# Handing over from the opening to the gather stream seven half turns earlier

## The chip, the cores and the metric

One core of a Trainium2 chip. The metric is the device time of one execution, in microseconds.

## The reference

One layer over 1024 prompt tokens and 64 sample tokens, float32, width 1024. Both kinds of token go through the mixer, then through the expert channel.

```python
xn = rmsnorm(x)                         # mixer
z = xn @ w_in                           # u (512), conv in (1024), gates (2048)
a = glu(gelu(s5(u)));  b = conv_module(z_conv) @ w_conv_out
x = x + (sigmoid(g_a) * a + sigmoid(g_b) * b) @ w_out
q = rmsnorm(x) @ w_q                    # 8 heads x 2 halves of 128
s1, s2 = q1 @ keys1.T, q2 @ keys2.T     # 128 scores each
v1, i1 = top_k(s1, 16);  v2, i2 = top_k(s2, 16)
sc, pos = top_k(v1[:, None] + v2[None, :], 16)    # 16 experts of 16384
coef = softmax(sc) * gelu(u_tab[e] @ xn)          # dot with the expert's u row
x = x + sum_k coef[k] * v_tab[e[k]];  y = rmsnorm(x)
```

So every token and head needs 16 expert rows of 8 KB (u and v side by side), gathered by index.

## The kernel before

**Two streams of work.** The mixer works on four groups of 272 tokens (256 of the prompt, 16 of the sample), channel-major. The expert channel works on nine tiles of 128 rows: tiles 0 to 7 are the prompt, two to a group, and tile 8 holds the sample tokens twice, half of the heads each. While the experts of group g are gathered, the mixer of group g+1 runs beside them.

**Turns.** A *slot* is one gathered block of 128 rows x 8 KB (1 MB), one expert per token of the tile. A *pair* is two heads, so 32 slots. A *turn* is 4 slots; 8 turns a pair (`PTURNS`), 32 turns a prompt tile, 64 turns a group, 272 turns in all (1088 slots). Each turn has two *half turns*, and the pieces of the mixer are dealt out to half turns by a table written by hand: `OPENING` for group 0, `STEADY` for groups 1 to 3. `mix_half` maps the running half-turn number to (h, group): the first `2 * SKEW` numbers go to the rest of the opening, h = OPEN, OPEN+1 and so on, and the next is h = 0 of group 1.

**The opening.** Half turns h = 0 to OPEN-1 of group 0 run with no slots beside them. All five engines walk the same list, each in its own program order, with semaphores between them. Late in it come: h 42 to 49, the eight `out` slabs (x + m @ w_out on TensorE, copied out by ScalarE with two instructions, L905 and L906); `rows`, the transposes of the result back to token rows (`token_rows`, TensorE L769, copied by `keep_rows`, VectorE L1317); `q`, sixteen query slabs, h 50 to 65 (16 matmul records of 272 columns, L591, copied by ScalarE into `qT`, L919); `score`, three key products (L708) which read that copy, one per query slab, copied out by `keep_scores` (L853, L854). ScalarE also does `sq` (sums of squares, L910, L911) and `rs` (L914, L916, after a root on GpSimd, L1608), which give `rst`, the row scale of the softmax and of `xn`.

**Choosing.** `made_top` (unit = 4 * head + 2 * half + tile) takes the top 16 of 128 scores with seven VectorE instructions; `tops` holds its half turns. `pair_top` takes the top 16 of 256 sums, `experts_of` turns positions into indices `idx` (L1439). `choose(n, r)` does both for the two heads of pair n in turns r = 2, 3, 6, 7 of the pair before. For pair 0 they are done in the opening, at h = CHOICE, both heads in a row. `exps` (ScalarE, Exp) and `weights` (VectorE) make the softmax weights `soft` of a pair.

**A slot's way.** GpSimd issues the gather (L1642) into one of 8 buffers (`RING`), two turns ahead, when TensorE has freed the buffer. VectorE does `dot` with `xn` (L1463), ScalarE `batch` for two slots (Gelu, coefficient, diagonal matrix: L945, L948, L952), TensorE `slots` multiplies the diagonal by the v half and accumulates (L779, four records a slot).

**Order inside a turn.** TensorE: mixer half turn, 2 slots, mixer half turn, 2 slots. VectorE the same, with dots, then `choose`. ScalarE: batch, half turn, batch, half turn. In turn 0 (and every 32nd) it differs: TensorE does both half turns before its four slots; VectorE does the half turn, `xn`, `weights`, four dots, and then the second half turn; and ScalarE does:

```python
if turn % 32 == 0:
    beside(2 * turn)
    pair_start(n, r)
    batch(n, TB * r)
...
batch(n, TB * r + 1)
...
beside(2 * turn + 1)
```

**PSUM.** The tiles of `q`, `score` and `out` share two banks in turn (`a_tile` waits until the tile before the last was copied out); `rows` uses three others (`v_tile`). SyncE loads each weight slab (512 KB) four ahead, when TensorE has finished with the buffer.

Of the kernel before, what the change touches and what calls it, by code (L numbers as in the profile page):

```python
# [90 lines left out]
class Plan:  # L91
# [20 lines left out]
    def due(self, step, h):  # L112
# [9 lines left out]
     "rows": [51, 52], "rest": [], "q": [50 + m for m in range(2 * HEADS)],  # L122
     "score": [51 + m for m in range(2 * HEADS)]},
# [4 lines left out]
     "cout": [38, 39, 40, 41], "rows": [52, 53], "sq": [53], "ms2": [54], "rs": [55],  # L128
     "tops": [52 + u // 2 for u in range(2 * HEADS)] + [64 + u for u in range(2 * HEADS)],
# [25 lines left out]
SKEW = 3  # L155
LAGS_AT = 12
CHOICE = 55
CHOSEN = 59
OPEN = 61
# [32 lines left out]
def program(nc, x_prompt, x_sample, kept, first, slabs, experts, g_ffn, g_final, x2_d, rs_d, score_d, made_d,  # L192
# [5 lines left out]
    with ExitStack() as ctx:  # L198
# [359 lines left out]
        def _(pe):  # L558
# [153 lines left out]
            def mix(h, g):  # L712
# [39 lines left out]
                for j in at("rows", h):  # L752
                    if j == 0:
                        a_emptied(a_at(g, "out", DT - 1))
                    token_rows(v_at(g, "rows", j), SPANS[2 * j])
# [7 lines left out]
            def token_rows(v, span):  # L763

                n, width = span
                for c in range(2):
                    out = v_tile(v + c)
                    for m in range(4):
                        last = pe.transpose(out[0:width, m * P:(m + 1) * P], outT[:, 4 * c + m, n:n + width], eye)  # L769
                    last.then_inc(v_ready, 1)  # L770
# [12 lines left out]
            def beside(number):  # L783

                if mix_half(number):
                    mix(*mix_half(number))
                g = rest_of("make", number)
                if g is not None:
                    token_rows(rest_v(g), SPANS[1])
# [22 lines left out]
        def _(act):  # L812
# [112 lines left out]

            def exps(n):

                act.wait_ge(best_done, 2 * n + 2)
                t = n // TPAIRS
                if t < TILES:  # L930
                    act.wait_ge(rst_ready, t + 1)
                else:
                    act.wait_ge(rs_in, 32)
                act.activation(neg_top[:, :], best[:, :, 0], ACT.Copy, scale=rst[:, t % 2, 1:2]).then_inc(neg_done, 1)
                act.wait_ge(neg_done, n + 1)
                for a in range(2):
                    act.activation(ex[:, a, :], best[:, a, :], ACT.Exp, bias=neg_top[:, a:a + 1],
                                   scale=rst[:, t % 2, 0:1],
                                   accum_out=den[:, a:a + 1]).then_inc(exp_done, 1)
# [14 lines left out]
            def pair_start(n, r):  # L954
                if r == 0:
                    act.wait_ge(soft_done, n + 1)
                if r == PTURNS - 1 and n < LAST_PAIR:
                    exps(n + 1)
# [41 lines left out]
            for h in range(OPEN):  # L1000
# [13 lines left out]
                if h == CHOSEN:  # L1014
                    exps(0)
                mix(h, 0)
            for turn in range(ALL_TURNS):
# [16 lines left out]
        def _(dve):  # L1034
# [423 lines left out]

            def dot(n, s0, s1):
# [63 lines left out]
            for h in range(OPEN):  # L1523
                if h == LAGS_AT:
                    setup_lags()
                mix(h, 0)
                for unit, g in tops_of(h - OPEN):
                    made_top(unit, g)
                if h == CHOICE:
                    for r in range(PTURNS):  # L1530
                        choose(0, r)
            dve.wait_ge(norms_in, 16)
            for turn in range(ALL_TURNS):
# [6 lines left out]
                if r == 0:  # L1540
                    weights(n)
                if turn % 32 == 0:
                    dot(n, STEPS * r, STEPS * (r + 1))
                    if ended_at(turn) is not None:
                        end(ended_at(turn))
                    if n < LAST_PAIR:
                        choose(n + 1, r)
                    beside(2 * turn + 1)
                else:
                    dot(n, STEPS * r, STEPS * r + BATCH)  # L1550
                    beside(2 * turn + 1)
                    dot(n, STEPS * r + BATCH, STEPS * (r + 1))
                    if n < LAST_PAIR:
# [204 lines left out]
```

## Time and profile before

| | |
|---|---|
| median of 3 runs | 3399.02 us (3393.8 to 3400.26) |
| profiled execution, first to last instruction | 3400.9 us (the page has no other time of it) |
| TensorE busy | 92% |
| VectorE / ScalarE / GpSimd busy | 71% / 36% / 42% |
| DMA | 1311.20 MB, mean 386 GB/s; 1140.92 MB of it in the gathers' queue |
| granted TensorE clock, mean | 0.985 |
| first gather issued | 289.22 us |
| first slot's matmuls | 315.71 us |
| half turn 0 of group 1 begins on TensorE | 352.60 us |

Instruction times in the timeline are starts from the beginning of the span. Consecutive instructions of a kind are merged; "x16" counts records. A float32 matmul leaves two records, so a query slab has 16 (eight products). "idle before <- X" is the time that the engine waited and what released it. The 4 us windows give the granted clock of just that stretch.

### The profile page before, as it was taken

What the parts mean: (1) busy time and instruction counts of PE and PEld (TensorE: products, weight loads), DVE (VectorE), ACT (ScalarE), POOL (GpSimd) and SP (SyncE); (2) the same over time, 40 slices, a digit from 0 to 9 for tenths busy, and PEclk for the clock granted to TensorE, in tenths of its full rate; (3) what the DMA queues carried; (4) which work ended last, traced back from release to release, by engine and by line L of the source; (5) the groups of instructions that cost most, each with busy time, mean ns of one, the idle gap of its engine ahead of it and who ended that gap; (6) DMA issues with size and microseconds to landing.
All of it is one profiled execution on the core that took longest, in us unless ns stands there. A gap on an engine that the chain in (4) does not pass through costs nothing.

```text
span 3400.9 us, 33356 instructions
## 1 busy us (share of the span) xinstructions
PE 3120.6 (92%) x10016; PEld 1785.7 (53%) x10016; DVE 2420.6 (71%) x5476; ACT 1218.7 (36%) x4064; POOL 1417.0 (42%) x1244
## 2 busy tenths in 40 slices
PE   8999999999999999999999999999998777777776
PEld 6877566555555565655554665655554223222232
DVE  8826998766578798665678798665688666666664
ACT  4323443343333443343334443333333333233332
POOL 1201355443344355343434454343434554454443
PEclk9999999999999999999999999999999999999999
DMA  4357999999999999999999999999999999999998
GB/s 133 103 181 284 369 403 418 419 411 419 417 402 416 405 415 417 418 412 418 412 415 413 396 418 413 394 419 419 412 410 384 420 420 420 394 420 420 419 403 341
DMA packets 209604, 1311.20 MB, mean 386 GB/s; under 512 B 23632, under 2 KB 28880, under 8 KB 70160
## 3 DMA queue, kind: packets, MB, share of 16 engines
q0 software_dynamic: 156672, 1140.92, 81.9%
q1 hardware_dynamic: 51472, 167.36, 13.0%
q8 instruction: 80, 1.31, 0.2%
q10 hardware_dynamic: 1280, 0.79, 0.1%
q14 instruction: 100, 0.82, 0.1%
HBM read 1298.34 MB, written 10.64 MB: 385 GB/s over the span
## 4 chain that ended last, share of the span: by engine, by line
PE 60%; DMA 21%; DVE 10%; issue 4%; ACT 3%; POOL 2%; POOLq 0%; DVEq 0%; SPq 0%; ACTq 0%
PE ps_acc L779 34%; DMA rows<-in_experts,idx 21%; PE ps_a L591 15%; DVE rows L1463 4%; PE ps_a L681 4%; PE ps_v L591 4%; POOL rows L1642 2%; PE ps_a L708 1%; PE ps_y L648 1%; ACT coef L948 1%; PE ps_a L685 1%; ACT diag L952 1%; PE ps_v L630 1%; DVE va L1297 1%; PE ps_v L692 0%
## 5 line engine op out<-in xcount | busy, mean ns | idle before, releaser
L779 PE MATMUL ps_acc<-rows,diag 128*128 128x512 f32 x4352 | 1998.5, 608 | 244.2 <-ACT diag L952 242.0
L1642 POOL DMA_INDIRECT rows<-in_experts,idx x1088 | 1290.5, 1186 | 1714.5 <-PE ps_acc L779 1377.6
L1463 DVE CUSTOM_DVE_ANT_0 rows<-rows,xn 128x1024 f32<-128x1024 f32 x1088 | 1324.9, 1230 | 776.3 <-DMA rows<-in_experts,idx 766.5
L779 PEld LDWEIGHTS ps_acc<-rows,diag 128*128 128x128 f32 x4352 | 818.2, 193 | 1275.6 <-issue 861.3
L945 ACT ACTIVATE act_v<-dots 128x2 f32<-128x2 f32 x544 | 110.6, 203 | 1789.6 <-DVE dots L1463 1787.7
L952 ACT ACTIVATE diag<-pk,coef 128x128 f32<-128x128 f32 x1088 | 377.2, 394 | 17.7
L591 PE MATMUL ps_a<-xnT,ring 128*128 128x272 f32 x1536 | 374.1, 399 | 0.9 <-issue 0.8
L591 PEld LDWEIGHTS ps_a<-xnT,ring 128*128 128x128 f32 x1536 | 295.9, 193 | 92.6 <-issue 33.9
L948 ACT ACTIVATE coef<-act_v,soft 128x1 f32<-128x1 f32 x1088 | 261.4, 287 | 17.8
L1297 DVE SCALAR_TENSOR_TENSOR va<-va,pk 128x302 f32<-128x302 f32 x480 | 258.8, 601 | 0.5
L591 PE MATMUL ps_a<-gates,ring 128*128 128x272 f32 x1024 | 246.3, 394 | 0.9 <-ACT gates L906 0.9
L591 PEld LDWEIGHTS ps_a<-gates,ring 128*128 128x128 f32 x1024 | 193.5, 190 | 63.0 <-issue 24.4
L681 PE MATMUL ps_a<-xnT,ring 128*128 128x272 f32 x512 | 130.3, 399 | 2.4 <-DVE xnT L1374 1.2
L591 PE MATMUL ps_v<-uy,ring 128*128 128x272 f32 x512 | 124.7, 392 | 0.0
L681 PEld LDWEIGHTS ps_a<-xnT,ring 128*128 128x128 f32 x512 | 94.5, 190 | 31.0 <-issue 11.5
L591 PEld LDWEIGHTS ps_v<-uy,ring 128*128 128x128 f32 x512 | 97.3, 190 | 24.9 <-issue 5.7
L1463 DVE DVE_READ_ACCUMULATOR2_ANT dots<- 128x1 f32 x1088 | 88.7, 82 | 0.0
L1608 POOL TENSOR_TENSOR rs<-rs,half 128x3 f32<-128x3 f32 x4 | 3.7, 931 | 153.9 <-DVE rs L1244 153.8
L591 PE MATMUL ps_a<-uy,ring 128*128 128x272 f32 x256 | 64.0, 393 | 0.5 <-ACT uy L839 0.5
L839 ACT ACTIVATE uy<-ps_a 32x68 f32<-32x68 f32 x256 | 56.0, 219 | 22.9 <-PE ps_a L591 19.9
L591 PE MATMUL ps_v<-xnT,ring 128*128 128x272 f32 x256 | 61.4, 393 | 0.0
L708 PE MATMUL ps_a<-pk,sig 128*128 128x128 f32 (+1 forms) x384 | 59.5, 276 | 0.0
(268 smaller groups left out, 2003.1 us busy)
## 6 DMA issues: line engine op xcount, KB each, us to landing
ring<-in_slabs SPq DMA_DIRECT2D x256, 512.0 KB
rows<-in_experts,idx POOLq DMA_INDIRECT x1088
ring<-made_slabs SPq DMA_DIRECT2D x24, 512.0 KB
xt<-in_x_prompt SPq DMA_DIRECT2D x4, 1024.0 KB, 13.2
out_y_prompt<-yt SPq DMA_DIRECT2D x8, 512.0 KB, 8.6
ring<-made_slabs SPq DMA_DIRECT2D x12, 256.0 KB
made_slabs<-rows SPq DMA_DIRECT2D x1, 2048.0 KB, 9.6
made_slabs<-rows SPq DMA_DIRECT2D x4, 512.0 KB, 9.3
```

Of the source, the lines that this page charges most:

```text
L591: last = pe.matmul(out[:, 0:N], w, rhs[:, k, :], start=(k == 0), stop=(k == kt - 1))
L630: last = pe.matmul(out[:, i * NK:(i + 1) * NK], w, uS[:, t, i * NK:(i + 1) * NK], start=True, stop=True)
L681: last = pe.matmul(out[:, 0:N], ring[:, slot, k * P:(k + 1) * P], merged[:, k, :], start=(k == 0), stop=(k == DT - 1))
L708: last = pe.matmul(out[0:width, t * KEYS:(t + 1) * KEYS], qT[:, m % 2, n:n + width], keys, start=True, stop=True)
L779: ins = pe.matmul(ps_acc[:, h, :], diag[:, slot, :], rows[:, slot, D + h * 512:D + (h + 1) * 512], start=first, stop=False, skip_group_che ...
L839: last = act.activation(o, x, func)
L945: act.activation(act_v[:, cols], dots[:, cols], ACT.Gelu).then_inc(gelu_done, 1)
L948: act.activation(coef[:, s:s + 1], act_v[:, s:s + 1], ACT.Copy, scale=soft[:, n % 2, s:s + 1]).then_inc(coef_done, 1)
L952: act.activation(diag[:, s % RING, :], shape, ACT.Copy, scale=coef[:, s:s + 1]).then_inc(diag_done, 1)
L1297: last = dve.scalar_tensor_tensor(acc[:, c, :], src, wk, acc[:, c, :], ALU.mult, ALU.add)
L1463: ins = dve.tensor_tensor_reduce(rows[:, slot, 0:D], rows[:, slot, 0:D], xn[:, :], 1.0, 0.0, ALU.mult, ALU.add, dots[:, s:s + 1])
L1642: pool.indirect_dma_start(out=rows[:, slot, :], out_offset=None, in_=experts, in_offset=bass.IndirectOffsetOnAxis(ap=idx[:, a, k:k + 1], a ...
```

## The change

Seven things move. The turns with slots begin at half turn 54, not 61, and `SKEW` goes from 3 to 6, so 12 half turns of the opening (54 to 65) lie beside slots instead of 6 (61 to 66), and group 1 begins at turn 6 instead of turn 3. `rows` moves from 51, 52 to 49, 50, ahead of the first query, and each half of it now waits only for the `out` slabs that it reads; `sq`, `ms2` and `rs` follow to 50 and 51. The scores of a head, both halves, are now made in one half turn, right behind the second query. The units of head 0 and 1 for tile 0 go first in `tops`. Head 0 of pair 0 is chosen at h = 51 and weighted by itself (`first_exps`, `first_weights`); head 1 is chosen in turns 0 and 1 and weighted in turn 3.

```diff
--- before.py
+++ after.py
@@ -119,14 +119,14 @@
      "s": [10, 12, 14, 16], "y": [15, 18, 21, 24],
      "gate": [13 + m for m in range(14)] + [35, 36], "glu": [27 + j for j in range(DT)],
      "mean": [29], "var": [31], "cout": [37, 38, 39, 40], "out": [42 + j for j in range(DT)],
-     "rows": [51, 52], "rest": [], "q": [50 + m for m in range(2 * HEADS)],
-     "score": [51 + m for m in range(2 * HEADS)]},
+     "rows": [49, 50], "rest": [], "q": [50 + m for m in range(2 * HEADS)],
+     "score": [51 + m - m % 2 for m in range(2 * HEADS)]},
     {"cp": [7, 9, 11, 13], "turn_in": [11, 13, 15, 17], "scan": [11, 13, 15, 17], "turn_back": [11, 13, 15, 17],
      "gelu": [16, 19, 22, 25], "tap": [10, 10, 12, 12, 14, 14, 16, 16] + [18 + u // 2 for u in range(24)],
      "glu": [28 + j for j in range(DT)],
      "centre": [30], "square": [30], "eps": [32], "root": [32], "scale": [33], "swish": [34],
-     "cout": [38, 39, 40, 41], "rows": [52, 53], "sq": [53], "ms2": [54], "rs": [55],
-     "tops": [52 + u // 2 for u in range(2 * HEADS)] + [64 + u for u in range(2 * HEADS)],
+     "cout": [38, 39, 40, 41], "rows": [49, 50], "sq": [50], "ms2": [51], "rs": [51],
+     "tops": [51, 54, 51, 55, 53, 57, 53, 58, 56, 60, 56, 61, 58, 62, 59, 63] + [64 + u for u in range(2 * HEADS)],
      "load_x": [59], "sq_next": [63], "ms_next": [64], "norm_next": [65]}, False, 0)
 STEADY = Plan(
     {"xn": [0, 1, 2, 3], "u": [9, 11, 21, 23], "cq": [5, 7, 13, 17], "cp": [6, 8, 15, 19],
@@ -152,11 +152,11 @@
 SLABS_0, SLABS_G = len(OPENING.slabs), len(STEADY.slabs)
 SLABS = SLABS_0 + (GROUPS - 1) * SLABS_G
 
-SKEW = 3
+SKEW = 6
 LAGS_AT = 12
-CHOICE = 55
-CHOSEN = 59
-OPEN = 61
+CHOICE = 51
+FIRST_EXPS = 3
+OPEN = 54
 ALL_TURNS = TILES * TPAIRS * PTURNS + SPAIRS * PTURNS
 LAST_PAIR = TILES * TPAIRS + SPAIRS - 1
 
@@ -750,9 +750,7 @@
                         pe.wait_ge(merged_done, DT * (g + 1))
                     out_slab(j, g)
                 for j in at("rows", h):
-                    if j == 0:
-                        a_emptied(a_at(g, "out", DT - 1))
-                    token_rows(v_at(g, "rows", j), SPANS[2 * j])
+                    token_rows(v_at(g, "rows", j), SPANS[2 * j], g)
                 for m in at("q", h):
                     if m == 0:
                         a_emptied(a_at(g, "out", DT - 1))
@@ -760,11 +758,12 @@
                 for m in at("score", h):
                     scores(m, g)
 
-            def token_rows(v, span):
+            def token_rows(v, span, g):
 
                 n, width = span
                 for c in range(2):
                     out = v_tile(v + c)
+                    a_emptied(a_at(g, "out", 4 * c + 3))
                     for m in range(4):
                         last = pe.transpose(out[0:width, m * P:(m + 1) * P], outT[:, 4 * c + m, n:n + width], eye)
                     last.then_inc(v_ready, 1)
@@ -786,7 +785,7 @@
                     mix(*mix_half(number))
                 g = rest_of("make", number)
                 if g is not None:
-                    token_rows(rest_v(g), SPANS[1])
+                    token_rows(rest_v(g), SPANS[1], g)
 
             pe.wait_ge(kept_in, 16)
             pe.sem_inc(slot_free, RING)
@@ -923,6 +922,15 @@
                     act.wait_ge(x_in, 32 * (g + 2))
                     squares()
 
+            def first_exps(a):
+
+                act.wait_ge(best_done, a + 1)
+                act.wait_ge(rst_ready, 1)
+                act.activation(neg_top[:, a:a + 1], best[:, a, 0:1], ACT.Copy, scale=rst[:, 0, 1:2]).then_inc(neg_done, 1)
+                act.wait_ge(neg_done, a + 1)
+                act.activation(ex[:, a, :], best[:, a, :], ACT.Exp, bias=neg_top[:, a:a + 1], scale=rst[:, 0, 0:1],
+                               accum_out=den[:, a:a + 1]).then_inc(exp_done, 1)
+
             def exps(n):
 
                 act.wait_ge(best_done, 2 * n + 2)
@@ -932,7 +940,7 @@
                 else:
                     act.wait_ge(rs_in, 32)
                 act.activation(neg_top[:, :], best[:, :, 0], ACT.Copy, scale=rst[:, t % 2, 1:2]).then_inc(neg_done, 1)
-                act.wait_ge(neg_done, n + 1)
+                act.wait_ge(neg_done, n + 2)
                 for a in range(2):
                     act.activation(ex[:, a, :], best[:, a, :], ACT.Exp, bias=neg_top[:, a:a + 1],
                                    scale=rst[:, t % 2, 0:1],
@@ -952,8 +960,12 @@
                     act.activation(diag[:, s % RING, :], shape, ACT.Copy, scale=coef[:, s:s + 1]).then_inc(diag_done, 1)
 
             def pair_start(n, r):
+                if n == 0 and r == FIRST_EXPS:
+                    first_exps(1)
+                if n == 0 and r == PTURNS // 2:
+                    act.wait_ge(soft_done, 2)
                 if r == 0:
-                    act.wait_ge(soft_done, n + 1)
+                    act.wait_ge(soft_done, n + 2 if n else 1)
                 if r == PTURNS - 1 and n < LAST_PAIR:
                     exps(n + 1)
 
@@ -1011,9 +1023,8 @@
                             last = act.activation(wt[W32 * k:W32 * (k + 1), i:PAIRS:CT, W32 * s:P],
                                                   lag[W32 * i:W32 * (i + 1), :, 0:width], ACT.Copy)
                     last.then_inc(wt_done, 1)
-                if h == CHOSEN:
-                    exps(0)
                 mix(h, 0)
+            first_exps(0)
             for turn in range(ALL_TURNS):
                 (n, r), t = divmod(turn, PTURNS), ended_at(turn)
                 if turn % 32 == 0:
@@ -1456,6 +1467,13 @@
                 dve.tensor_tensor(soft[:, n % 2, :].rearrange("p (a k) -> p a k", a=2), ex[:, :, :],
                                   inv[:, :].unsqueeze(2).to_broadcast([P, 2, TOPK]), ALU.mult).then_inc(soft_done, 1)
 
+            def first_weights(a):
+
+                dve.wait_ge(exp_done, a + 1)
+                step(dve.reciprocal(inv[:, a:a + 1], den[:, a:a + 1]))
+                dve.tensor_scalar(soft[:, 0, a * TOPK:(a + 1) * TOPK], ex[:, a, :], inv[:, a:a + 1], None,
+                                  ALU.mult).then_inc(soft_done, 1)
+
             def dot(n, s0, s1):
                 for s in range(s0, s1):
                     slot = s % RING
@@ -1527,8 +1545,8 @@
                 for unit, g in tops_of(h - OPEN):
                     made_top(unit, g)
                 if h == CHOICE:
-                    for r in range(PTURNS):
-                        choose(0, r)
+                    pair_top(0, 0)
+                    experts_of(0, 0)
             dve.wait_ge(norms_in, 16)
             for turn in range(ALL_TURNS):
                 n, r = divmod(turn, PTURNS)
@@ -1537,12 +1555,16 @@
                 beside(2 * turn)
                 if turn % 32 == 0:
                     start(turn // 32)
-                if r == 0:
+                if n == 0 and r in (0, FIRST_EXPS):
+                    first_weights(r // FIRST_EXPS)
+                if r == 0 and n:
                     weights(n)
                 if turn % 32 == 0:
                     dot(n, STEPS * r, STEPS * (r + 1))
                     if ended_at(turn) is not None:
                         end(ended_at(turn))
+                    if n == 0:
+                        pair_top(0, 1)
                     if n < LAST_PAIR:
                         choose(n + 1, r)
                     beside(2 * turn + 1)
@@ -1550,6 +1572,8 @@
                     dot(n, STEPS * r, STEPS * r + BATCH)
                     beside(2 * turn + 1)
                     dot(n, STEPS * r + BATCH, STEPS * (r + 1))
+                    if (n, r) == (0, 1):
+                        experts_of(0, 1)
                     if n < LAST_PAIR:
                         choose(n + 1, r)
                 if turn > 32 and turn % 32 == 1:
```

## Rows read from the trace of the kernel before

**Rows 1.** The page: transfers in 40 slices, and the chain that ended last.

```profile
DMA  4357999999999999999999999999999999999998
...
PE 60%; DMA 21%; DVE 10%; issue 4%; ACT 3%; POOL 2%; POOLq 0%; DVEq 0%; SPq 0%; ACTq 0%
```

**Rows 2.** Stretches of 100 us: busy times, granted clock, DMA share, GB/s.

```profile
core 0: us, PE busy (x) PEld busy (x) DVE busy (x) ACT busy (x) POOL busy (x), PEclk, DMA share, GB/s
300.00:400.00 100.00, 94.38 (x338) 57.06 (x337) 78.75 (x241) 41.39 (x134) 31.07 (x28) 1.00 0.98 386
...
2800.00:2900.00 100.00, 76.78 (x160) 30.05 (x160) 63.96 (x127) 34.50 (x112) 47.41 (x41) 0.97 1.01 420
```

**Rows 3.** Stretches of 4 us in the first turns, same columns.

```profile
292.00:296.00 4.00, 4.00 (x19) 3.37 (x20) 3.73 (x13) 0.66 (x3) 3.08 (x4) 1.00 0.98 400
...
340.00:344.00 4.00, 4.00 (x19) 3.23 (x18) 3.83 (x13) 1.38 (x5) 2.15 (x2) 1.00 0.66 212
```

**Rows 4.** Line 1491, at the start of turns 224 and 256: durations, then first and last start.

```profile
L1491 DVE SCALAR_TENSOR_TENSOR xn<-x2t,rst,gf x1: 1277/1277/1277, 2897.7 to 2897.7; 128x1024 f32<-128x1024 f32 x1
...
L1491 DVE SCALAR_TENSOR_TENSOR xn<-x2t,rst,gf x1: 1284/1284/1284, 3226.8 to 3226.8; 128x1024 f32<-128x1024 f32 x1
```

**Rows 5.** VectorE in order of time: start, duration, line, idle before.

```profile
264.01 0.29 DVE L1391 MAX8 topv<-gp 128x8 f32<-128x128 f32 x1 [4.15 <-ACT gp L854]
...
265.85 0.29 DVE L1391 MAX8 topv<-gp 128x8 f32<-128x128 f32 x1
...
282.54 0.43 DVE L1417 TENSOR_TENSOR hot<-topv 128x256 f32<-128x256 f32 x1
...
288.08 0.18 DVE L1439 SCALAR_TENSOR_TENSOR idx<-part 128x16 uint32<-128x16 f32 x1
...
331.07 0.17 DVE L1244 TENSOR_SCALAR rstd<-ssq 128x3 f32<-128x3 f32 x1 [13.36 <-ACT hst L821]
```

**Rows 6.** TensorE in order of time, half turns 50 to 66 of the opening.

```profile
254.17 3.93 PE L591 MATMUL ps_a<-gates,ring 128*128 128x272 f32 x16 [0.87 <-ACT gates L906]
...
257.94 1.04 PE L769 MATMUL ps_v<-pk,gates 128*128 128x128 f32 x8
...
273.38 3.93 PE L591 MATMUL ps_a<-gates,ring 128*128 128x272 f32 x16
...
278.01 3.93 PE L591 MATMUL ps_a<-gates,ring 128*128 128x272 f32 x16
...
315.71 7.13 PE L779 MATMUL ps_acc<-rows,diag 128*128 128x512 f32 x16 [0.53 <-ACT diag L952]
...
322.68 3.83 PE L591 MATMUL ps_a<-gates,ring 128*128 128x272 f32 x16
...
336.60 3.70 PE L779 MATMUL ps_acc<-rows,diag 128*128 128x512 f32 x8 [1.26 <-ACT diag L952]
...
352.60 0.38 PE L600 MATMUL ps_a<-pk,va 128*128 128x128 f32 x2
```

**Rows 7.** GpSimd in order of time: the first gather.

```profile
289.22 1.19 POOL L1642 DMA_INDIRECT rows<-in_experts,idx  x1 [14.88 <-DVE idx L1439]
```

**Rows 8.** Line 455, the load of x: issue to landing, four transfers.

```profile
DMA to landing us min/median/max: 5.4/13.2/14.8
```

**Rows 9.** ScalarE in order of time.

```profile
270.28 1.06 ACT L910 ACTIVATE va<-x2t 128x1024 f32<-128x1024 f32 x1 [0.90 <-ACT gp L854]
...
313.21 1.28 ACT L945 ACT_TABLE_LOAD   x1 [2.01 <-DVE dots L1463]
...
317.19 0.38 ACT L919 ACTIVATE sig<-ps_a 128x272 f32<-128x272 f32 x1
```

**Rows 10.** Stretches of 4 us around a stop of TensorE at 110 us.

```profile
108.00:112.00 4.00, 2.10 (x14) 1.56 (x12) 3.83 (x10) 3.45 (x15) 0.21 (x1) 1.00 0.44 145
112.00:116.00 4.00, 4.00 (x22) 3.77 (x22) 4.00 (x7) 0.00 (x0) 2.70 (x3) 0.63 0.06 23
116.00:120.00 4.00, 4.00 (x10) 2.95 (x10) 4.00 (x7) 0.00 (x0) 3.40 (x5) 0.52 0.00 0
```

## Prediction

> **What bounds the kernel now.** I read four views in this order: the page, stretches of 100 us and 4 us, the timeline of each engine between 250 and 355 us, and single lines where a turn begins.
>
> The page shows two resources near their limit at once. The transfers fill nearly every slice from 300 us on, yet the chain that ended last lies 60% on TensorE and only 21% on transfers [rows 1]. The stretches part the two. At the end, with no mixer beside the slots, TensorE is busy 77% and the transfers run at 420 GB/s: there the gathers bound. In the first turns TensorE is busy 94% and the transfers reach 386 GB/s [rows 2]. In 4 us stretches: 400 GB/s when eight gathers have just been issued, but 212 GB/s at 340 us, where TensorE works all the time, the eight buffers are full, and no new gather can be issued until it frees one [rows 3]. So where query slabs run beside slots, TensorE bounds.
>
> Hence two prices. A turn without mixer costs (3226.8 - 2897.7) / 32 = 10.28 us [rows 4]. The same four slots cost TensorE 322.68 - 315.71 = 6.97 us [rows 6]; a query slab with its score costs it 278.01 - 273.38 = 4.63 us [rows 6].
>
> **The change, part by part.**
>
> *Where it acts.* From half turn 0 of group 1 on, table, costs and order are the same in both kernels, and only eight buffers carry anything over. So I take that stretch as equally long, and need two numbers: when TensorE reaches that half turn (352.60 us now [rows 6]), and what is left behind it. Left are three turns fewer, and they go missing at the end, where the mixer is over: 3 x 10.28 = 30.8 us. The change wins if TensorE gets there less than 30.8 us later.
>
> *`rows` ahead of the query.* The two transposes cost 1.04 us each [rows 6] and are only moved. The last `out` is done at about 253.3 us, since query 0 now waits 0.87 us to 254.17 [rows 6] for its copy. New: first half of the transposes inside that wait, the second behind it, then the sample rows, query 0 at 255.5, and by query 4 TensorE stands at 273.7 against 273.38 now: +0.3 us. ScalarE's `sq` now stands in front of the copy of query 0 (2.2 us from 270.28 [rows 9]), with the store of the sample rows ahead of it: it starts at about 257.2 and ends at 259.4, when query 0 has just ended. GpSimd's root and `rs` end at 261.4, before query 1 ends at 262.9. Covered; with slower row copies the scores would slip by as much.
>
> *The first gather.* Scores 0 and 1 come out of TensorE at 263.8 and 264.6, ScalarE has copied them at 264.5 and 265.4. Two units of `made_top` at 265.85 - 264.01 = 1.84 us each [rows 5] end at 268.3; `pair_top` with `experts_of` took 288.26 - 282.54 = 5.7 us [rows 5]: index at 274.0. Plus 0.96 us as now (288.26 to 289.22 [rows 5, 7]): gather at 275.0, 14.2 us earlier.
>
> *Turn 0, the new wait.* TensorE does half turns 54 and 55 and then the slots. In 55 lie query 5, score 4 and score 5, and score 5 needs ScalarE's copy of query 5. ScalarE makes that copy in its second half turn, behind both batches, and the second batch needs dots 2 and 3, so gathers 2 and 3. Now it is already so late (copy of query 12 at 317.19, after the batches [rows 9]), but there the half turn's score belongs to the query before and nobody waits. Query 5 ends at 281.1, score 4 at 281.9. Gather 0 lands no sooner than 275.0 + 5.4 = 280.4, the shortest time to landing of a load of that size [rows 8]. Gather 3 is three times 1.05 MB later, 2.5 us each at 420 GB/s [rows 2], and two slabs share the engines, 1.25 us each: 290.4. Dot, batch and copy: 1.15 + 1.4 + 0.5, so score 5 starts at about 293.4: TensorE stands 11.5 us. Bounds: 8 us if no slab shares (and dot 3 waits for nothing else), 15 us if the landing is as slow as the median 13.2 us of that load [rows 8], which was under full traffic. I take 11.5, since the engines are nearly empty at 275 us. Behind the copy on ScalarE wait the copies of scores 4 and 5, and behind these VectorE's units 8 and 10 in turn 1; they end at 299.3, before TensorE needs dots 4 and 5. The Gelu table load of 1.28 us [rows 9] is under the wait for gather 1.
>
> *Second head in turns 0, 1 and 3.* VectorE's work is the same plus two small instructions; it has room (12 of the 16 us of a turn). But ScalarE's `first_exps` in turn 3 loads the Exp table and then Gelu again, 1.28 us each, and comes only after the copy of score 9: I get dots 12 and 13 at 335.5, their diagonal at 338.3, TensorE free at 336.4: 1.9 us, 0 to 4.
>
> *Squares of the next x.* ScalarE does these 3.3 us at h = 63, behind scores 12 and 13, and VectorE waits for them before any dot (13.36 us now, which leads to a TensorE wait of 1.26 us [rows 5, 6]). After: VectorE waits until 367.3 in turn 5, dots 20 and 21 at 371.8, diagonal at 373.4, TensorE free at 370.4: 3.0 us, 1 to 5.
>
> *TensorE's ledger, query 4 to group 1.* Before: 12 queries with scores 55.6, one more score 0.9, three turns of slots 20.9, waits 0.53 + 1.26 = 1.8: 79.2, as the trace has it (352.60 - 273.38 [rows 6]). After: 55.6, six turns of slots 41.8, waits 11.5 + 1.9 + 3.0 = 16.4: 113.8, from 273.7: 387.5 us, so 34.9 us later than before.
>
> *The clock.* A stop as long is not cheap afterwards. At 110 us TensorE stood some 2 us and then ran 8 us at a granted 0.63 and 0.52, half of the time and more at 1.2 GHz [rows 10]; that lost 4 x (0.37 + 0.48) = 3.4 us. The waits of 0.5 to 1.3 us in the first turns cost nothing (clock 1.00 [rows 2]). I add 3.4 us for turn 0 and nothing for turns 3 and 5; bounds 0 and 7.
> The Trainium skill, TensorE: Matmul & The Clock Gate, section Why this matters for your kernels, says that an idle gap between bursts of matmuls brings the array back to half clock; by this rule the wait of turn 5 would fall under it too, and the sum would be some 3 us higher. The trace agrees for the 2 us stop at 110 us.
>
> *Credit.* In the first half turns of group 1 VectorE bounds (two units and four dots a turn), and it now enters them with nothing in hand, since its 13.36 us wait came 21.5 us before. After, by the sums above, it is some 3.5 us ahead of TensorE, less one more unit: I credit 3 us, 0 to 4.
>
> Sum: 34.9 + 3.4 - 3.0 - 30.8 = +4.5 us on 3400.9, so 3405.4. The three timed runs have a median 1.9 us below this profiled span: 3403.5, I say 3403.
>
> **Rivals.**
> 1. *The stream simply starts 14.2 us earlier*, and all of it is kept: 3399 - 14 = 3385. For it: transfers at 0.98 and above from 300 us on [rows 1, 2]. Against it: 212 GB/s with full buffers [rows 3]; a turn with two queries costs TensorE 16 us, the transfers 12.5.
> 2. *The ledger holds, but turn 0 hardly waits*: gathers 0 to 3 land together, as eight are in flight at once, the wait is 4 us and brings no clock loss: 3403 - 7.5 - 3.4 = 3392. Against it: 2.5 us for each megabyte is the transfers' limit.
> 3. *Every odd half turn waits as turn 0 does.* In 57, 59, 61, 63 and 65 the second score also needs the copy of that half turn's query, behind batch 2r + 1. It decides once the second pair of dots of a turn ends less than 2 us before the query does. By my times it is 4 to 7 us ahead. If not: 3 us in each of five, one clock loss more: 3403 + 15 = 3418.
> 4. *The chain to the first index does not get shorter*, since `sq` and `rs` hold up the score copies on ScalarE: each us there moves the gather and the wait of turn 0, up to 5 us: 3408.
>
> **How the numbers follow.** The ledger with its waits 0.55, rival 1 0.15, rival 2 0.12, rival 3 0.12, rival 4 0.06. With the low bounds (8 us, 0, 1, no clock loss, 4 us credit) the ledger gives 3403.5 - 3.5 - 3.9 - 3.4 - 1 = 3392; with the high ones (15, 4, 5, 7, 0) 3403.5 + 3.5 + 4.1 + 3.6 + 3 = 3418. Its own likely range is 3396 to 3410. The range to hold 8 in 10 is 3388 to 3412. The runs before differ by 0.19%, so I call anything within 0.2% (6.8 us, 3392.2 to 3405.8) no change. Faster: rivals 1 and 2, 0.26. Slower: rivals 3, 4 and a quarter of the ledger, 0.31. Same: the rest, 0.43.
>
> **What would show it.** First gather near 275 us; TensorE standing some 11 us in turn 0, ended by ScalarE's copy of query 5, with the granted clock below 1 behind it; group 1's half turn 0 on TensorE at 387 to 391 us; a stretch behind it as long as before; three turns fewer of 10.28 us. Wrong would be: a later index, a stop much shorter than 8 us, transfers over 400 GB/s through turns 2 to 5, or a different length of the stretch with the mixer.

## The result: 0.18% slower, and where it stands in the profile

Over 20 runs each, the changed kernel takes 3404.02 us (3395.92 to 3412.18) and the kernel before 3398.18 us (3392.09 to 3401.12): a ratio of 1.0018, 95% interval [1.0011, 1.0024], some 6 us. The forecast was 3403, with "no change" the likeliest case and "slower" next. The profiled execution of the changed kernel took 3400.72 us, with a span of 3398.6. That is one of its quicker ones, while the 3400.9 us span of the kernel before is one of its slower ones, so the two traces by themselves do not show the 6 us; the timed runs do.

The page of the changed kernel (engine's busy time; transfers in 40 slices; chain by engine). Against [rows 1] the slices of the transfers hardly differ, and the chain has less of TensorE and more of VectorE:

```profile
PE 3115.1 (92%) x10016; PEld 1783.4 (52%) x10016; DVE 2428.5 (71%) x5478; ACT 1222.0 (36%) x4067; POOL 1417.0 (42%) x1244
...
DMA  4358999999999999999999999999999999999998
...
PE 56%; DMA 20%; DVE 13%; issue 5%; ACT 3%; POOL 2%; POOLq 0%; DVEq 0%; ACTq 0%; SPq 0%
```

One thing must be taken off first. The opening's code is the same up to half turn 48, but in this trace it ran 3.3 us ahead. This is no effect of the change: a second trace of the kernel before has the slab at 209.24 us, 5.4 us ahead of its first. The first `out` slab on TensorE, kernel before, then after:

```profile
214.62 0.72 PE L681 MATMUL ps_a<-xnT,ring 128*128 128x272 f32 x2 [1.20 <-DVE xnT L1374]
```

```profile
211.32 0.72 PE L681 MATMUL ps_a<-xnT,ring 128*128 128x272 f32 x2 [1.21 <-DVE xnT L1385]
...
252.21 7.50 PE L591 MATMUL ps_a<-gates,ring 128*128 128x272 f32 x32
...
270.63 7.60 PE L591 MATMUL ps_a<-gates,ring 128*128 128x272 f32 x32
278.07 0.93 PE L708 MATMUL ps_a<-pk,sig 128*128 128x128 f32 x6
291.00 1.73 PE L708 MATMUL ps_a<-pk,sig 128*128 128x128 f32 x6 [12.00 <-ACT sig L918]
292.66 9.37 PE L778 MATMUL ps_acc<-rows,diag 128*128 128x512 f32 x16
301.87 3.83 PE L591 MATMUL ps_a<-gates,ring 128*128 128x272 f32 x16
...
337.82 3.70 PE L778 MATMUL ps_acc<-rows,diag 128*128 128x512 f32 x8
...
372.78 3.70 PE L778 MATMUL ps_acc<-rows,diag 128*128 128x512 f32 x8 [2.44 <-ACT diag L960]
...
385.34 0.38 PE L600 MATMUL ps_a<-pk,va 128*128 128x128 f32 x2
```

Here and below I count from that slab. Group 1's half turn 0 comes 385.34 - 211.32 = 174.0 us behind it, and 352.60 - 214.62 = 138.0 before: +36.0 us, while the three turns that go missing at the end save 30.8. The second fence holds all of it (the TensorE rows answer to [rows 6]): queries 2 to 5 and their scores run on without a gap until score 4 at 278.07; then TensorE stands 12.00 us, released by ScalarE's copy of query 5 (line L918). Score 5 then takes 1.66 us (291.00 to 292.66) instead of about 0.86, and the slots of turn 0 take 9.21 us (292.66 to 301.87) instead of 6.97. The slots at 337.82 (turn 3) wait for nothing; those at 372.78 (turn 5) wait 2.44 us for a diagonal.

Why the copy came so late stands on two other engines. ScalarE, then VectorE, in turn 0:

```profile
282.29 1.28 ACT L953 ACT_TABLE_LOAD   x1 [7.29 <-DVE dots L1481]
283.59 0.20 ACT L953 ACTIVATE act_v<-dots 128x2 f32<-128x2 f32 x1
...
289.13 0.20 ACT L953 ACTIVATE act_v<-dots 128x2 f32<-128x2 f32 x1 [4.11 <-DVE dots L1481]
...
290.48 0.37 ACT L918 ACTIVATE sig<-ps_a 128x272 f32<-128x272 f32 x1
```

```profile
280.98 1.23 DVE L1481 CUSTOM_DVE_ANT_0 rows<-rows,xn 128x1024 f32<-128x1024 f32 x1 [1.98 <-DMA rows<-in_experts,idx]
...
284.75 1.22 DVE L1481 CUSTOM_DVE_ANT_0 rows<-rows,xn 128x1024 f32<-128x1024 f32 x1 [2.54 <-DMA rows<-in_experts,idx]
...
287.87 1.23 DVE L1481 CUSTOM_DVE_ANT_0 rows<-rows,xn 128x1024 f32<-128x1024 f32 x1 [1.88 <-DMA rows<-in_experts,idx]
```

Dots 1, 2 and 3 each waited for their gather, and start 3.8 and 3.1 us apart; after dot 3 follow the batch at 289.13 and, only behind it, the copy at 290.48. GpSimd issued the first of these gathers 17.8 us earlier than in [rows 7], 14.5 without the head start:

```profile
271.42 1.19 POOL L1666 DMA_INDIRECT rows<-in_experts,idx  x1 [14.24 <-DVE idx L1450]
```

Stretches of 4 us (columns as in [rows 2]). The clock goes to 0.50, the lower of its two levels (1.2 GHz), while TensorE stands, and stays there through 288 to 296 us although TensorE works again from 291. The transfers fall to 135 GB/s at the end of turn 0 and to 192 GB/s as turn 2 begins, as in [rows 3]; that the eight buffers were full then is read from the program's order:

```profile
280.00:284.00 4.00, 0.00 (x0) 0.00 (x0) 1.23 (x2) 1.67 (x3) 2.60 (x2) 0.94 1.01 415
284.00:288.00 4.00, 0.00 (x0) 0.00 (x0) 1.36 (x3) 1.00 (x4) 0.00 (x0) 0.50 1.03 431
288.00:292.00 4.00, 1.00 (x4) 0.93 (x4) 3.72 (x11) 2.07 (x8) 0.00 (x0) 0.50 1.00 420
292.00:296.00 4.00, 4.00 (x7) 1.64 (x7) 3.51 (x18) 0.53 (x2) 0.00 (x0) 0.50 1.01 420
296.00:300.00 4.00, 4.00 (x9) 1.72 (x8) 3.83 (x11) 0.00 (x0) 1.53 (x2) 0.85 0.48 135
...
316.00:320.00 4.00, 4.00 (x15) 2.49 (x14) 3.86 (x12) 1.38 (x5) 2.44 (x2) 1.00 0.55 192
```

Line 1509, at the start of turns 224 and 256; a turn at the end costs 10.27 us, as in [rows 4]:

```profile
L1509 DVE SCALAR_TENSOR_TENSOR xn<-x2t,rst,gf x1: 1277/1277/1277, 2896.8 to 2896.8; 128x1024 f32<-128x1024 f32 x1
...
L1509 DVE SCALAR_TENSOR_TENSOR xn<-x2t,rst,gf x1: 1283/1283/1283, 3225.4 to 3225.4; 128x1024 f32<-128x1024 f32 x1
```

### The profile page after: what moved, and what is told of

The parts are those of the page before. It is cut to its first block, busy times and chain, and to the rows that moved or that the text cites. A ratio compares the mean times of both kernels' runs of the same rounds, so it can differ in the third digit from the quotient of the medians.

```text
span 3398.6 us, 33383 instructions
## 1 busy us (share of the span) xinstructions
PE 3115.1 (92%) x10016; PEld 1783.4 (52%) x10016; DVE 2428.5 (71%) x5478; ACT 1222.0 (36%) x4067; POOL 1417.0 (42%) x1244
## 4 chain that ended last, share of the span: by engine, by line
PE 56%; DMA 20%; DVE 13%; issue 5%; ACT 3%; POOL 2%; POOLq 0%; DVEq 0%; ACTq 0%; SPq 0%
PE ps_acc L778 31%; DMA rows<-in_experts,idx 20%; PE ps_a L591 14%; DVE rows L1481 5%; PE ps_a L681 4%; PE ps_v L591 3%; POOL rows L1666 2%; DVE va L1308 1%; PE ps_a L708 1%; ACT coef L956 1%; ACT diag L960 1%; PE ps_a L685 1%; PE ps_y L648 1%; ACT uy L838 0%; PE ps_v L692 0%
## 5 line engine op out<-in xcount | busy, mean ns | idle before, releaser
L956 ACT ACTIVATE coef<-act_v,soft 128x1 f32<-128x1 f32 x1088 | 261.5, 287 | 17.8
L1308 DVE SCALAR_TENSOR_TENSOR va<-va,pk 128x302 f32<-128x302 f32 x480 | 267.1, 618 | 0.3
```

The source lines that it names most:

```text
L956: act.activation(coef[:, s:s + 1], act_v[:, s:s + 1], ACT.Copy, scale=soft[:, n % 2, s:s + 1]).then_inc(coef_done, 1)
L1308: last = dve.scalar_tensor_tensor(acc[:, c, :], src, wk, acc[:, c, :], ALU.mult, ALU.add)
```

## The experiments

All are timed in turn with the kernel before in the same job (5 to 12 runs of each). The table gives, from the first `out` slab, the time to group 1's half turn 0 (h0) and to the row transposes at its h = 4, each with its distance from break-even: that is the time of the kernel before (138.0 and 160.4), plus 10.28 us for each turn that the kernel has more ahead of group 1. The expectations count from query 0, which `rows` now delays by 1.3 us.

| kernel | SKEW | to h0 | vs break-even | to h = 4 | vs break-even | ratio to before |
|---|---|---|---|---|---|---|
| before again | 3 | 137.8 | -0.2 | 160.3 | -0.2 | 0.9993 [0.9984, 1.0002] |
| changed | 6 | 174.0 | +5.2 | 193.2 | +1.9 | 1.0018 [1.0011, 1.0024] |
| changed again | 6 | 173.9 | +5.1 | 193.1 | +1.8 | 1.0035 [1.0021, 1.0048] |
| copy first | 6 | 174.6 | +5.8 | 192.7 | +1.5 | 1.0038 [1.0024, 1.0052] |
| filled wait | 6 | 171.7 | +2.9 | 190.9 | -0.4 | 1.0026 [1.0014, 1.0037] |
| dots first | 6 | 169.9 | +1.1 | 188.1 | -3.2 | 1.0008 [0.9999, 1.0017] |
| three waits less | 6 | 164.3 | -4.5 | 184.1 | -7.1 | 0.9998 [0.9989, 1.0006] |
| the same, filled | 6 | 167.2 | -1.6 | 187.0 | -4.3 | 1.0003 [0.9993, 1.0013] |
| changed, slots at 61 | 3 | 143.7 | +5.7 | 167.4 | +7.0 | 1.0013 [1.0004, 1.0022] |
| three waits less, at 61 | 3 | 144.7 | +6.7 | 169.8 | +9.4 | 1.0020 [1.0011, 1.0029] |
| slots at 61, squares at 62 | 3 | 139.4 | +1.5 | 162.9 | +2.4 | 0.9988 [0.9976, 1.0001] |
| before, squares at 62 | 3 | 136.6 | -1.4 | 161.9 | +1.5 | 0.9993 [0.9985, 1.0002] |
| three waits less, at 56 | 5 | 158.5 | -0.1 | 176.6 | -4.4 | 0.9978 [0.9969, 0.9986] |

**Does the early stream alone gain?** Slots back at 61, all else as changed:

```diff
-SKEW = 6
-OPEN = 54
+SKEW = 3
+OPEN = 61
```

> The changed kernel with the slots beginning at half turn 61 and SKEW 3 again: rows, scores, head-wise choice and the early first index stay, so the first eight gathers are issued some 14 us earlier than in the kernel before, but no slot's matmuls are. Theory (TensorE's ledger): its work up to group 1 is that of the kernel before, so the time is that of the kernel before, 3398 us within 3. Rival (the transfers bound, an earlier first gather is a gain of its own): up to 14 us faster, 3385. Second rival (rows, head-wise weights or the score order cost something themselves): slower than the kernel before by 3 us or more.

The first gather is issued at 271.47 us, as early as in the changed kernel, and the time is 1.0013: nothing gained, so rival 1 falls. It is even slower, as the second rival of the expectation has it: the squares of the next x now stand behind two scores in one half turn. TensorE, turns 0 and 1:

```profile
315.34 7.03 PE L778 MATMUL ps_acc<-rows,diag 128*128 128x512 f32 x16
...
337.50 5.40 PE L778 MATMUL ps_acc<-rows,diag 128*128 128x512 f32 x8 [2.44 <-ACT diag L960]
```

The wait in turn 1 is 2.44 us instead of 1.26 [rows 6], and the 8 records behind it take 5.40 us instead of 3.70.

With the squares one half turn earlier (`"sq_next": [63]` to `[62]`) most of that is gone:

> The changed kernel with the slots beginning at half turn 61 (SKEW 3) and only the squares of the next x one half turn earlier; ScalarE's order is left as it is, so that turn 0 has no other wait. Break-even from query 0 to group 1 is 98.4 us. Theory (ledger): 102.95 us without the earlier squares, of which 2.4 are the wait in turn 1 and 1.7 the half clock behind it: 98 to 99 us, the time of the kernel before within 0.001. Rival: rows, scores by head and the weights of head 1 cost something of their own, 101 us or more.

139.4 us to h0 against 143.7, and 0.9988 against 1.0013. Inside the interval that is the time of the kernel before: head-wise choice, `rows` and scores cost 1.5 us at h0 and nothing that can be measured in the whole time. The same edit on the kernel before:

> The kernel before with nothing changed but the squares of the next x one half turn earlier. Theory: VectorE's wait of 13.4 us in front of dots 6 and 7 shrinks to about 4 and TensorE's 1.26 us with it: 96 to 97 us from query 0 to group 1, 1 to 2 us faster. Rival: VectorE bounds turns 3 and 4 anyway, 98 us and no change.

TensorE's 1.26 us wait is gone and h0 comes 1.4 us sooner, as expected. By h = 4 it had given back 2.9 us, but not to VectorE: behind the same wait of 1.96 us as in the kernel before (for ScalarE's copy), the next 8 records take 6.31 us instead of 3.70, and the granted clock is 0.50 from 360 to 364 us.

```profile
360.44 6.31 PE L779 MATMUL ps_acc<-rows,diag 128*128 128x512 f32 x8
```

In time it is 0.9993, inside the interval, so the run does not decide between theory and rival.

**The wait of turn 0.** ScalarE copies first:

```diff
                 if turn % 32 == 0:
                     beside(2 * turn)
+                    if turn == 0:
+                        beside(1)
                     pair_start(n, r)
                     batch(n, TB * r)
...
-                beside(2 * turn + 1)
+                if turn:
+                    beside(2 * turn + 1)
```

> The changed kernel, but in turn 0 ScalarE copies query 5 and scores 4 and 5 before its two batches, so score 5 waits for no gather. Theory (TensorE's ledger): TensorE no longer stands 12 us in front of score 5; it waits some 5 us for the diagonals of slots 0 and 1 and 2 us for slots 2 and 3, and its four slots of turn 0 end 8 us earlier (about 23 us after query 5 ended, 15 instead); group 1 begins 8 us earlier and the whole takes 3404 - 8 = 3396 us, 0.998 of the kernel before. Rival (the time is lost later, since the gathers or the mixer stretch bound it): group 1 may begin earlier but the time stays at 3402 to 3406.

The expectation missed. The 12 us wait is gone, but not one microsecond at h0. TensorE, and VectorE behind dot 3:

```profile
286.07 9.91 PE L778 MATMUL ps_acc<-rows,diag 128*128 128x512 f32 x16 [4.49 <-ACT diag L960]
295.82 3.83 PE L591 MATMUL ps_a<-gates,ring 128*128 128x272 f32 x16
302.73 6.68 PE L778 MATMUL ps_acc<-rows,diag 128*128 128x512 f32 x8 [3.08 <-ACT diag L960]
...
373.06 5.40 PE L778 MATMUL ps_acc<-rows,diag 128*128 128x512 f32 x8 [2.44 <-ACT diag L960]
```

```profile
290.39 0.42 DVE L1431 TENSOR_TENSOR hot<-topv 128x256 f32<-128x256 f32 x1
...
293.47 0.29 DVE L1405 MAX8 topv<-gp 128x8 f32<-128x128 f32 x1
...
299.11 1.23 DVE L1484 CUSTOM_DVE_ANT_0 rows<-rows,xn 128x1024 f32<-128x1024 f32 x1
```

Instead of one wait there are two, 4.49 us before slots 0 and 1 and 3.08 before slots 4 and 5, with half clock behind each: it costs 2.8 us in the row at 286.07 (9.91 instead of 7.13) and 3.0 in the row at 302.73 (6.68 instead of 3.70). The second wait is VectorE's: from 290.39 to 299.11 it chooses head 1 and does three units before dot 4. Waits and half clock together are 13.3 us, against 15.0 (12.00, 0.8 and 2.2) for the one wait in the changed kernel. The 1.7 us between them went in turn 5, where the 8 records behind the same 2.44 us wait took 5.40 us and not 3.70. So the wait for the copy had a second owner right behind it.

The clock by itself, with the wait filled:

```diff
+                if (m, g) == (5, 0):
+                    pe.wait_ge(y_gelu, CT)
+                    for k in range(26):
+                        pe.matmul(ps_y[:, 0:N], par("eye"), x2T[:, k % DT, :], start=True, stop=True)
                 out = a_tile(a_at(g, "score", m))
```

> The changed kernel with 26 products of an identity with query input put in front of score 5, into a PSUM bank that nobody reads then: TensorE works through the wait of turn 0 instead of standing. It adds work and takes none away. Theory (the clock is part of the cost): granted clock 1.00 from 280 to 300 us after the opening's offset, the 16 records of slots 0 to 3 take 7.1 us and not 9.4, and the time falls by 3 us to 3401. Rival (the stop itself is all the cost): no change or up to 1 us slower, 3404 to 3405.

```profile
279.39 12.19 PE L707 MATMUL ps_y<-gates,pk 128*128 128x272 f32 x52
291.85 1.00 PE L712 MATMUL ps_a<-pk,sig 128*128 128x128 f32 x6 [0.28 <-ACT sig L922]
292.79 7.13 PE L782 MATMUL ps_acc<-rows,diag 128*128 128x512 f32 x16
```

The row of slots behind it takes 7.13 us against 9.37, and the granted clock is 1.00 from 276 to 304 us: the products kept the clock up. TensorE worked 12.2 us for nobody and came 2.3 us sooner to h0. In time it is 1.0026 against 1.0035 of the changed kernel in the same job; the intervals overlap, so the expected 3 us are shown at h0 alone.

Then VectorE's share was moved too:

```diff
-"tops": [51, 54, 51, 55, 53, 57, 53, 58, 56, 60, 56, 61, 58, 62, 59, 63]
+"tops": [51, 54, 51, 55, 53, 57, 53, 58, 57, 60, 57, 61, 58, 62, 59, 63]
...
-                    if n == 0:
-                        pair_top(0, 1)
...
                     if (n, r) == (0, 1):
+                        pair_top(0, 1)
                         experts_of(0, 1)
```

> The changed kernel with the copy of query 5 ahead of the batches, and VectorE's choice of head 1 behind dots 6 and 7 of turn 1 and its units 8 and 10 one half turn later, so that dots 4 and 5 follow dot 3 after one unit. Measure: from the start of query 0 to half turn 0 of group 1 on TensorE (98.4 us in the kernel before, whose turns 0 to 2 stand against turns 0 to 5 here, so 98.4 + 30.85 = 129.3 is break-even; the changed kernel has 133.1 in two traces). Theory (the wait of turn 0 has two owners, ScalarE's copy and, right behind it, VectorE's load): no wait before slots 4 and 5, 127 to 128 us, 5 us faster than the changed kernel. Rival (gather landings alone set slots 4 and 5): 133 us, as with the copy alone.

4.1 us less to h0 (169.9), 129.1 us from query 0 where 127 to 128 were expected, no wait before slots 4 and 5, and 1.0008. Next, the squares at 62 on top:

> The kernel of dots first, and the squares of the next x on ScalarE one half turn earlier (62), so that VectorE no longer waits for them in turn 5. Theory (ledger: each TensorE wait removed comes off the time): 123 to 124 us from query 0 to group 1, that is 5 to 6 us under break-even, 0.998 of the kernel before, 10 us under the changed kernel. Rival (what is won ahead of group 1 is lost behind it, where transfers and buffers bound): 123 us there, but a time within 3 us of the kernel before.

```profile
284.39 9.91 PE L778 MATMUL ps_acc<-rows,diag 128*128 128x512 f32 x16 [4.59 <-ACT diag L960]
294.13 3.83 PE L591 MATMUL ps_a<-gates,ring 128*128 128x272 f32 x16
297.80 3.60 PE L778 MATMUL ps_acc<-rows,diag 128*128 128x512 f32 x8
```

One long wait is left, for the diagonals of slots 0 and 1 (another in turn 2 is 0.51 us). Gather 1 sets it: dot 1 starts at 280.58 us, when that gather has landed, and Gelu's table load of 1.28 us (from 281.89) and the batch follow. To h0 it is as expected, 9.7 us under the changed kernel. In time it is 0.9998, not 0.998, as the rival had it. A filler in the wait that is left did harm:

> The kernel with three waits less, and 12 products of an identity in the wait that is left in turn 0, into a PSUM bank that nobody reads then. Theory (half clock is part of the price of a wait): slots 0 to 3 take 7 to 8 us with the clock at 1.00 instead of 9.9, 121 to 122 us from query 0 to group 1, 2 us faster than with three waits less. Rival: the clock falls anyway or the filler delays the slots, 124 us.

The products stood in front of score 5 and so of ScalarE's copy and batch: slots 0 to 3 started 4.7 us later, and h0 came 2.9 us later.

**The move of the slots.** At 61 again, and at 56:

> The same kernel with the slots beginning at half turn 61 and SKEW 3, to price the move of the slots by itself. Theory: three turns of slots cost TensorE 20.9 us beside query slabs and 30.8 at the end, so without the move, and without the first wait of turn 0, it takes 97 us from query 0 to group 1 and the time is 4 to 5 us above that of the kernel with three waits less. Rival (the move is worth nothing since VectorE and the transfers fill the stretch anyway): equal times.

This run tells little of the move: with the copies first, the squares of half turn 62 stand before the batches of turn 0, and TensorE waits 6.05 us for the first diagonal. It took 104.0 us to h0 from query 0 instead of the expected 97.

```diff
-SKEW = 6
-OPEN = 54
+SKEW = 5
+OPEN = 56
```

> The kernel with three waits less, with the slots beginning at half turn 56 (SKEW 5), one turn later. By TensorE's ledger the first slots then come at about 291 us, when gathers 0 to 3 have landed, so no wait and no half clock in turn 0; one turn of slots fewer stands ahead of group 1. Theory: 123.6 - 7.0 - 8 = 108 to 110 us from query 0 to group 1 against a break-even of 98.4 + 20.6 = 119.0, so 9 us under it, and, since the kernels with SKEW 6 came out some 4 us above their ledger, 0.998 of the kernel before. Rival (whatever comes earlier is given back behind group 1): 1.000.

This is the best kernel here, 0.9978 [0.9969, 0.9986], median 3393.7 us, 7.8 us under the kernel before in its job (3401.49). But not by the sum that I gave. It came to h0 at 158.5 us, 9 us later than forecast, since two waits were new:

```profile
283.58 9.29 PE L591 MATMUL ps_a<-gates,ring 128*128 128x272 f32 x32 [2.16 <-ACT uy L853]
...
298.09 5.40 PE L778 MATMUL ps_acc<-rows,diag 128*128 128x512 f32 x8 [3.49 <-ACT diag L960]
```

```profile
283.00 0.39 ACT L852 ACTIVATE uy<-ps_a 128x256 f32<-128x256 f32 x1 [2.87 <-remote]
...
295.59 1.28 ACT L953 ACT_TABLE_LOAD   x1 [0.42 <-ACT uy L853]
```

The second comes from the copies of queries 6 and 7 and their scores in front of the batches: the four dots are done at 292.58, the copies at 295.20 (Gelu's table load comes only at 295.59). The first, on the copy of score 4, was released by something "remote", outside the engines; what it is, no run tells.

**The two kernels again**, for the spread:

> The changed kernel itself once more, for a second trace on this chip and as the mark for the others: 3404 us, 1.002 of the kernel before; a wait of 12 us in turn 0; the stretch from group 1's half turn 0 to the end as long as in the kernel before less 31 us, within the noise of two traces.

> The kernel before once more: ratio 1.000 within 0.0015, 98.4 us from query 0 to group 1, and a second value for the stretch from group 1 to the end (3048.3 us in its first trace; the four traces of the changed kernel and its kin, three turns added back, have 3044 to 3058).

From the first `out` slab to h = 4 each repeats within 0.2 us. The changed kernel came out at 1.0035 here and at 1.0018 in its first job; the intervals overlap. The rest repeats less well: from h = 4 to the end, three turns added back, the changed kernel takes 3024.9 and 3038.4 us, the kernel before 3025.9 and 3024.5. Nor does the opening: the first slab comes at 214.62 and 209.24 us in the kernel before, and between 209.2 and 214.6 in all fourteen traces. The two traces of the kernel before part at 67 us, where TensorE stands 2.96 us in the first and 1.20 in the second. The next slab behind that stop, first trace and second:

```profile
70.96 6.12 PE L591 MATMUL ps_a<-xnT,ring 128*128 128x272 f32 x16
```

```profile
68.28 3.88 PE L591 MATMUL ps_a<-xnT,ring 128*128 128x272 f32 x16
```

The granted clock is 0.58 and 0.57 from 68 to 76 us in the first and 1.00 in the second.

## Why the prediction held, step by step

- **First gather.** Forecast 14.2 us earlier, measured 14.5.
- **`rows`.** Forecast +0.3 us at query 4; 270.63 - 211.32 against 273.38 - 214.62 is +0.55.
- **Turn 0.** Forecast 11.5 us and the engine that ends it; measured 12.00 and that engine. Shown by copy first, and there the step was incomplete: it called the time of dots 4 and 5 covered, and it was covered only by the wait itself. Gelu's table load came behind dot 1 (282.29) and not under the wait for gather 1; it lay under the waits for gathers 2 and 3 instead, and cost nothing.
- **Turn 3.** Forecast 1.9 us, measured 0. The clock loss of turn 0 is not what hid it: with the wait filled and the clock at 1.00 there is none either, and the row starts where the query before it ends:

```profile
335.71 3.70 PE L782 MATMUL ps_acc<-rows,diag 128*128 128x512 f32 x8
```

What was too long in the forecast is ScalarE's chain. It had dots 12 and 13 at 335.5, some 6.3 us behind the end of score 9 (TensorE free at 336.4, less a query and 8 records); in the trace dot 12 starts 3.6 us behind it (334.20), and Gelu's table load (333.78) runs beside the dots.
- **Turn 5.** Forecast 3.0, measured 2.44 (2.45 in the second trace). Shown by the squares at 62.
- **Clock.** Forecast 3.4 us. In the rows it is 0.8 for score 5 and 2.2 for the slots, 3.0. Filling the wait saved 2.3 to h0, and there the score began 0.6 us later.
- **To h0.** Forecast 34.9 + 3.4 = 38.3 us later, measured 36.0, with the 3.3 us of the opening taken off.
- **Credit for VectorE's lead.** Forecast 3; from h0 to h = 4 it is 22.4 us before and 19.2 after: 3.3. But it does not last. Group 2's half turn 0, before and after:

```profile
1103.17 0.38 PE L600 MATMUL ps_a<-pk,va 128*128 128x128 f32 x2
```

```profile
1135.55 0.38 PE L600 MATMUL ps_a<-pk,va 128*128 128x128 f32 x2
```

From one h0 to the next it is 750.6 us before and 750.2 after, and over all traces 750.5 to 753.1 with SKEW 3 and 748.6 to 754.2 with SKEW 6. So the credit was true at h = 4 and gone by group 2.
- **Three turns fewer.** 10.28 us each before, 10.27 after.
- **"That stretch as equally long."** This step was off, by how much depends on where one counts from. From h = 4 to the end, turns added back, six traces with SKEW 3 have 3019 to 3028 us, mean 3024.7; seven with SKEW 6 have 3025 to 3038, mean 3031.5; the one with SKEW 5 has 3023.1. So SKEW 6 takes some 7 us more behind h = 4. Some 4.7 of these are what it had won between h0 and h = 4 (19.1 us against 23.7 in the mean) and gives back. From h0 on the means are 3048.5 and 3050.5, 2.0 apart, with 2.7 and 4.4 us of spread; within that, the stretch from group 2's h0 to group 3's is 3.5 us longer (755.3 against 751.8). The timed runs, which hold more executions, show more: what a kernel loses by its ratio, in us, less its distance at h0 is +1 to +7 for the seven kernels and runs with SKEW 6, -6 to 0 for those with SKEW 3, and -7 for SKEW 5. So SKEW 6 pays something behind group 1's h0, between 2 and 6 us, and three waits less, 4.5 us under break-even at h0, came out level with the kernel before. What it consists of is open: group 1's half turns meet other turns (the one that begins a tile has h = 52 or 116 beside it, not 58 or 122), and ScalarE and VectorE have another order there; no run tests it.
- **Rivals.** Rival 1 fell with slots at 61. Rival 2 (a short wait) fell with the trace. Rival 3 did not come: in half turns 57 to 65 the second score follows at once. Rival 4 did not come: the copies were in time.

The forecast's sum, 3403, thus holds two errors of opposite sign: 2.3 us too much ahead of group 1, and too little behind it, by the mean of the seven traces some 5 us (3050.5 against 3048.3 less the credit of 3). What is left, some 3 us, lies within the spread of one kernel's runs (3395.92 to 3412.18 us); the same kernel had a median of 3411.34 us in its second job. That the first median came so near to 3403 is in part luck.

## What to carry to other kernels

When work is moved from before a stream to beside it, keep the ledger of the engine that is full in both places: a turn moved is worth its price at the end less its price here (10.28 - 6.97 = 3.3 us), and the one wait of 12.00 us at the join ate more than the three turns gave. A wait has as many owners as there are paths that end at about that time: name the next one before you remove the first. And if a score needs a copy that stands behind batches which wait for a transfer, the order on the copying engine can hold TensorE back however early the first index is known. Put the copy first, and the next path takes over: here nothing was won at h0 until VectorE's order moved too.

## What the runs showed of the hardware

A filler of useless matmuls in a 12 us stop kept the granted clock at 1.00, and TensorE was 2.3 us sooner at h0; whether it pays in the whole time these runs do not tell. Waits of nearly the same length do not cost the same. The 2.44 us of turn 5 cost nothing more in the changed kernel (3.70 us for the 8 records behind it, clock 1.00 from 372 to 380 us), and 1.7 us more in copy first and dots first (5.40 us). A stop of 1.46 us in group 1 was followed by 5.40 us for 8 records too (slots at 61, squares at 62), and one of 1.96 us by 3.70 us in one kernel and 6.31 in another. In the second trace of the changed kernel such a stop fell in the mixer stretch, on TensorE and in stretches of 4 us:

```profile
2022.14 6.32 PE L778 MATMUL ps_acc<-rows,diag 128*128 128x512 f32 x8 [2.42 <-ACT diag L960]
```

```profile
2020.00:2024.00 4.00, 1.85 (x2) 0.84 (x3) 4.00 (x9) 1.38 (x5) 0.00 (x0) 0.58 1.02 421
2024.00:2028.00 4.00, 4.00 (x7) 1.68 (x6) 3.93 (x11) 2.91 (x13) 0.94 (x1) 0.57 0.85 336
```

Eight records took 6.32 us, and 8 us ran at 0.58 and 0.57. A stop thus does not always cost the same. In the opening of the kernel before this goes with a part of the 5.4 us between its two traces; how large a part it has in the spread of whole runs, these runs do not tell.
The Trainium skill, TensorE: Matmul & The Clock Gate, section Why this matters for your kernels, says that idle gaps between bursts of matmuls bring the array back to half clock, and warns of gaps longer than the stops of 2.4 us here. These traces agree for the stops of 12 and 4.5 us. They also show half clock behind some stops of 1.5 to 2.4 us, of which the section does not warn, and none behind others of that length.
